# In seven of eight head pairs the weighed values of the step two back are multiplied ahead of the step's scores

## What is computed

```python
def one_chunk(c):
    start = c * CHUNK
    q_c = lax.dynamic_slice_in_dim(q, start, CHUNK, axis=1)
    k_c = lax.dynamic_slice_in_dim(kpad, start, BAND, axis=1)
    v_c = lax.dynamic_slice_in_dim(vpad, start, BAND, axis=1)
    s = jnp.einsum('bqhd,bkhd->bhqk', q_c, k_c).astype(jnp.float32) * scale + bias
    valid = (start - REACH + jnp.arange(BAND)) >= 0
    s = jnp.where(valid, s, NEG)
    p = jax.nn.softmax(s, axis=-1).astype(v.dtype)
    return jnp.einsum('bhqk,bkhd->bqhd', p, v_c)
```

## Time and profile before

| | |
|---|---|
| Median of 3 runs | 2588.9 us (2586.3 to 2588.97) |
| Profiled execution | 2589.23 us, of which 2587.4 us are the span from first to last instruction |
| TensorE matmul busy | 2517.3 us (97%) |
| VectorE, ScalarE, GpSimd busy | 1558.9, 874.7, 232.4 us |
| Granted TensorE clock, mean | 0.990 |
| The seven main pairs | some 70 to 590 us of the span |

### The profile page before, as it was taken

The page is one execution under the profiler, slowest core; times in us unless marked ns, Lnnn a source line. Parts: engine busy times, 40 slices in busy tenths (PEclk is TensorE's granted clock), DMA queues, the critical chain, the costliest instruction groups (busy, mean ns, idle before and its releaser), DMA issues.

```text
span 2587.4 us, 42752 instructions
## 1 busy us (share of the span) xinstructions
PE 2517.3 (97%) x16343; PEld 2425.6 (94%) x16343; DVE 1558.9 (60%) x2978; ACT 874.7 (34%) x1645; POOL 232.4 (9%) x521
## 2 busy tenths in 40 slices
PE   7999999998899999999999999999999999999998
PEld 7888888886799999999999899999999999999998
DVE  4566666566766666666666524244666666666666
ACT  5433334443622222223332530233323332222223
POOL 0000000000400000000000420222000000000003
PEclk9999999999899999999999998999999999999999
DMA  6111111100011011111111110111111111111112
GB/s 154 43 36 45 49 39 41 47 30 19 33 50 49 32 49 49 49 49 49 49 49 33 51 49 17 46 37 49 49 50 49 49 49 49 49 42 39 33 49 77
DMA packets 101508, 121.23 MB, mean 47 GB/s; under 512 B 3900, under 2 KB 90084, under 8 KB 101412
## 3 DMA queue, kind: packets, MB, share of 16 engines
q1 hardware_dynamic: 97892, 109.91, 13.1%
q0 software_dynamic: 2864, 7.88, 1.3%
q10 hardware_dynamic: 656, 2.12, 0.2%
HBM read 109.49 MB, written 10.40 MB: 46 GB/s over the span
## 4 chain that ended last, share of the span: by engine, by line
PE 89%; DVE 4%; POOL 2%; ACT 2%; issue 1%; DMA 0%; POOLq 0%; ACTq 0%; DVEq 0%
PE psum L160 26%; PE psum L162 26%; PE psum L161 26%; PE psum L904 3%; PE psum L884 3%; PE psum L869 2%; POOL total L231 2%; PE psum L1703 1%; DVE gx_lo L219 1%; PE psum L777 0%; ACT conv_t L1387 0%; PE psum L1691 0%; DVE gx_lo L1862 0%; DVE conv_t L1452 0%; DMA xin<-in_x_prompt 0%
## 5 line engine op out<-in xcount | busy, mean ns | idle before, releaser
L160 PE MATMUL psum<-gx_hi,w_hi 128*128 128x352 f32 x3264 | 1069.1, 328 | 22.5 <-DVE w_lo L1277 10.4
L161 PE MATMUL psum<-gx_lo,w_hi 128*128 128x352 f32 x3264 | 1057.6, 324 | 0.0
L162 PE MATMUL psum<-gx_hi,w_lo 128*128 128x352 f32 x3264 | 1056.8, 324 | 0.0
L160 PEld LDWEIGHTS psum<-gx_hi,w_hi 128*128 128x128 f32 x3264 | 616.9, 189 | 30.1 <-issue 13.2
L161 PEld LDWEIGHTS psum<-gx_lo,w_hi 128*128 128x128 f32 x3264 | 617.1, 189 | 0.8 <-issue 0.7
L162 PEld LDWEIGHTS psum<-gx_hi,w_lo 128*128 128x128 f32 x3264 | 616.9, 189 | 0.0
L1479 DVE TENSOR_TENSOR x<-x,psum 128x352 f32<-128x352 f32 x528 | 258.7, 516 | 121.9 <-PE psum L162 121.9
L1387 ACT ACTIVATE conv_t<-a_gate,cur 128x352 f32<-128x352 f32 x132 | 90.2, 683 | 534.1 <-DVE a_gate L1444 533.9
L160 PE MATMUL psum<-h_hiA,w_hi 128*128 128x352 f32 x528 | 172.8, 327 | 4.3 <-DVE x L1479 4.3
L160 PE MATMUL psum<-h_hiB,w_hi 128*128 128x352 f32 x528 | 172.1, 326 | 0.0
L162 PE MATMUL psum<-h_hiB,w_lo 128*128 128x352 f32 x528 | 171.7, 325 | 0.0
(11 more groups left out here) (187 smaller groups left out, 3206.9 us busy)
## 6 DMA issues: line engine op xcount, KB each, us to landing
raw<-in_f_w_up SPq DMA_DIRECT2D x44, 1024.0 KB, 5.0
raw<-in_f_w_down SPq DMA_DIRECT2D x22, 1024.0 KB, 4.8
raw<-in_a_w_qkv SPq DMA_DIRECT2D x24, 512.0 KB, 3.8
raw<-in_b_w_in SPq DMA_DIRECT2D x8, 1024.0 KB, 5.5
raw<-in_a_w_o SPq DMA_DIRECT2D x8, 512.0 KB, 3.3
raw<-in_b_w_out SPq DMA_DIRECT2D x4, 1024.0 KB, 5.1
out<-raw SPq DMA_DIRECT2D x6, 512.0 KB, 2.6
xin<-in_x_prompt SPq DMA_DIRECT2D x4, 512.0 KB, 8.5
```

The source lines that it names most:

```text
L160: pe.matmul(out, w[0], rhs[0], start=first, stop=False)
L161: pe.matmul(out, w[0], rhs[1], start=False, stop=False)
L162: return pe.matmul(out, w[1], rhs[0], start=False, stop=last)
```

## The change

In the rounds of the seven main pairs, `weigh` of step s - 2 is issued ahead of `scores` of step s instead of behind it. The last pair keeps its order. Nothing else is touched.

```diff
             for s in range(STEPS + 2):
+                if s >= 2 and not late:
+                    weigh(t, par, s - 2)
                 if s < STEPS:
                     scores(t, par, s)
                     if late and s < 4:
                         late_wo(t, s, 0)
-                if s >= 2:
+                if s >= 2 and late:
                     weigh(t, par, s - 2)
                 if s == STEPS and not (at_pair(t, LAST - 1)):
                     wo_tiles(t, 0, KT)
```

## The result

The changed kernel takes 2617.2 us (median of 5, 2615.2 to 2618.4) against 2586.95 for the kernel before on the same chip (2586.3 to 2589.0): a ratio of 1.0116, with a 95% interval of 1.0105 to 1.0127. It is slower by 1.2%; the forecast was 2617.

The account below looks back on a forecast made before the run. TensorE, busy 97% of the span, was taken to bound the kernel, so its new stalls are paid in full: 2589.2 us plus 28 us of uncovered waits, other terms at no cost, gives 2617. Range 2608 to 2629.

Parts of the forecast that it names:

- Part 1, the uncovered wait: Weighing in rounds 3 to 8 waits for ScalarE's copy of the extra, formerly beside the scores: 4.0 us per pair, 28 us.
- The low end, 0.05: Faster signal from copy's end to TensorE, 0.05 us instead of 0.11: each of 42 stalls 0.06 shorter, 25.5 us in all.
- Part 2, the seams: Loader's rests between matmul groups; the unseen weighing-to-scores seam taken as equal, no cost; 0.05 us on 49 is 2.5 us either way.
- Part 3, the chain: Scores, maximum, exponentials and scaling start about 1.0 us later; ScalarE's room just fits, at no cost; otherwise 1.5 us in all.
- Part 4, the pair's end: TensorE's 1.1 us wait for VectorE's addition in the output projection moves along unchanged; nothing counted.
- The clock: TensorE's clock stays at 1.00 in the pairs; rival that it falls: 2629 or 2689 us, 7%.
- faster: Rival: earlier weighing lets VectorE's additions start ahead, removing the 1.1 us wait in 7 pairs: 8 us, 2581; 2%.
- absorbed: Rival: stalls taken back at each pair's end, where TensorE would meet the same VectorE wait: 2589 to 2594; 4%.
- half the stalls: Rival: the extras' copies start sooner or the signal is faster, so stalls cost 14 us: 2603; 7%.

Follow-up runs that it names:

- round 2 alone: Against the kernel before, the new order only in round 2 of the main pairs, the one changed round with no extra ahead of it: 2586.33 us, ratio 0.9998.
- the early extra: Changed kernel with the extra's transposes issued six matmuls earlier, ahead of the projection's last two tiles: 2593.21 us; the same in the old order: 2587.12 us.
- the moved split: Kernel before with VectorE's weight split moved behind the eighth addition to x: 2579.96 us; the same edit with the new order: 2609.54 us.

## Why the prediction was right

- *What bounds.* TensorE had no stall in the pairs that the new order could remove; nothing was won, and the runs with round 2 alone and with the early extra show that nothing was lost by the order itself either.
- *Part 1, the uncovered wait,* carried the sum and held: 4.2 us per pair for 4.0 forecast. The difference has its place. I took 0.11 us from the end of a copy to TensorE's start, which is the loader's start; the first matmul starts another 0.03 later (262.29 and 262.32), and 42 x 0.03 is 1.3 us. So the 27.9 that seven times 3.99 come to and 1.3 make 29.2, and the seven pairs became 29.5 longer; by the starts of the groups the six stalls are 0.63, 0.85, 0.85, 0.52, 0.85 and 0.51. The low end, 0.05, was the form of wait that stands on the load itself. In the changed trace line 893's wait is an instruction of its own (262.21 to 262.26), ahead of the load at 262.29, so 0.11 was the right row.
- *Part 2, the seams.* The unseen one, weighing to scores, leaves the loader idle for 0.17 us, as its neighbours do. The 0.05 either way weren't needed.
- *Part 3, the chain.* Its size came out as worked: in round 6 of the changed kernel the split ends and the copy starts in this order:

```profile
277.34 1.07 ACT L679 ACTIVATE w_hi<-raw 128x1024 fp32r<-128x1024 f32 x1
278.51 0.60 ACT L788 ACTIVATE kout<-psum 128x512 f32<-128x512 f32 x1
279.25 1.31 PE L904 MATMUL psum<-pT,v 128*64 128x128 f32 x20 [0.78 <-ACT kout L788]
```

  By the recorded ends 0.10 us of room are left of 1.04. Back to back, ScalarE starts the copy 0.11 before the recorded end of the split (267.70 + 1.06 against 268.65 in the run with the early extra), so the real room is 0.2. "At no cost" was right by that little, and the run with the early extra shows what comes behind that point.
- *Part 4, the pair's end.* Unchanged at 1.1 us. That it hangs on the split was argued from the order of VectorE's work; the moved split has now shown it, and that it cost 1.4 us a pair.
- *The clock.* It stayed at 1.00 in the pairs, with six stalls in each of the seven. What the Trainium skill tells of another kernel (TensorE: Matmul & The Clock Gate, A second HAM failure mode), that short idle times between groups of matmuls made the clock swing, did not come true here for stalls of 0.4 to 0.8 us in rounds of 8 us. The rivals faster, absorbed and half the stalls were all wrong: the copies start as far behind the transposes as before.
- *By luck,* in part: against the median of the kernel before, 2586.95, the changed one lost 30.3 us, 29.5 of them in the pairs, and the sum had 28. The forecast started from an execution of 2589.2, 2.3 us above that median, with a sum 2.3 too small, and the two met.

## What to carry to other kernels

A wait costs by where it stands, not by what it waits for: before two groups of work on the bounding engine are swapped, list the waits of the one that moves ahead, and ask for each which instruction releases it and what ran in between. Here the producer's copy, of 0.6 us at the longest, was hidden by 1.28 us of other matmuls, and the swap put the consumer right behind it, 42 times. Where an engine does wait, moving work into the gap helps only if that work is released earlier than what the engine waits for; and a small repeated wait of another cause (a weight split ahead of urgent additions) was worth 7 us, where the order had nothing to win.

## What was not expected of the hardware

Behind line 893's wait the first matmul starts 0.03 us after its weight load (262.29 and 262.32), where the weighing before started with it (252.74 and 252.75). It isn't idle time as such that does it: behind the idle 1.24 us at 640.89 in the last pair, where the wait stands on the load itself, the matmul starts with its load. Why is open.

```profile
640.89 0.66 PE L904 MATMUL psum<-pT,v 128*64 128x128 f32 x8 [1.24 <-ACT pT L1001]
```

And VectorE's additions, recorded at 0.51 to 0.52 us each, start closer together than that. In the run with the later split they do so every 0.48 us (eight end 3.89 us after the first start, the last taking 0.52), as fast as TensorE makes the tiles. Where they had been held up by the split, in the kernel before, they follow each other faster still:

```profile
285.86 1.37 DVE L1127 TENSOR_TENSOR x<-x,psum 128x352 f32<-128x352 f32 x3
```

The last of the three takes 0.51, which leaves 0.43 us from each start to the next. VectorE has room at the pair's end; the durations alone would have made it the slower of the two.
